# First attention of a two-layer diffusion backbone: sums of squares as two rounded matrix products

## The chip, the cores and the metric

The kernel runs on one core of one Trainium2 chip. The metric is the device time of one execution in microseconds (us), as the median over several runs. One core has TensorE (PE, matrix products into PSUM), VectorE (DVE), ScalarE (ACT), GpSimd (POOL, which works on SBUF only), and SyncE (SP), which issues the DMAs. Each engine has a queue of its own that it works through in order, and engines wait for each other by semaphores.

## What is computed

The model has two layers. The first one mixes 1024 latent tokens and 256 context tokens by multi-head attention with 12 heads beside a Fourier mixing; the second by windowed attention beside pooling. After each comes a gated convolutional FFN. The change touches the first attention alone. What it computes per head is, cut to what matters:

```python
kv = (rmsnorm(ckv, ckv_g) @ w_ukv).reshape(B, L, A_HEADS, A_NOPE + A_V)
k = jnp.concatenate([kv[..., :A_NOPE], broadcast(k_rope)], axis=-1)    # 64 + 32 = 96 entries
k = rmsnorm(k, k_g)
q = rmsnorm((rmsnorm(cq, cq_g) @ w_uq).reshape(B, L, A_HEADS, A_QK), q_g)
q, k = rope_tail(q, cos, sin), rope_tail(k, cos, sin)
p = softmax(q @ k.T * A_QK ** -0.5)      # over context and latent keys
o = p @ v
```

So each head needs, for each of its 1280 keys and 1280 queries, the sum of 96 squares (the mean in `rmsnorm`). This sum over partitions is a matrix product with a matrix of ones.

## The kernel before, in words

Function `heads0` holds the first attention. The tokens lie along the free dimension, in three chunks `CH` of 512, 512 and 256 columns. A head is worked off in 11 passes u = 0 to 10 of half-steps v = 2u and 2u + 1. In pass u TensorE computes the logits of the next 128 keys against 1024 queries (`qk`, lines 2423 to 2425: two blocks of 512 columns, each as three products of halves that are rounded to the type fp32r: high x high, high x low, low x high), ScalarE takes the exponentials (line 2629), GpSimd adds them up (`add`, lines 2400 to 2405), and TensorE multiplies them with the values (`pv`, line 2455, in plain float32). The three exponential buffers `pr[u % 3]` come free when both `pv` and `add` of their pass are done.

Between this work, in half-steps 2 to 18, the same engines prepare the *next* head, in steps that `steps_at(v)` names. There are six pieces w = 0 to 5: three chunks of keys (w < 3), three of queries. For each piece:

- `project` (TensorE, lines 2492 and 2496, plain float32): keys or queries in PSUM bank `PB[w]`.
- `project` (ScalarE): for keys a scaled copy `kx` (line 2577) and the square `sk` (2579), for queries the square `sq` (2586), for w = 5 also a plain copy (2584).
- `squares` (TensorE, line 2506, plain float32): ones x squares into bank `NB[w % 2]`.
- `inverse` (ScalarE): logarithm (2595), then exponential with factor -0.5 (2598), so the inverse root, back into the bank.
- `unit` (VectorE, 2675, 2687 and 2690, 2681): the normed result, with the rotation for queries, whose first part is `turn` (2698, 2701) and reads the projection in PSUM.
- `high` (ScalarE, 2606) rounds the result to fp32r, `low` (VectorE, 2709) takes the rest, `cast` (GpSimd, 2393) makes a bfloat16 copy.

Then come the maxima (half-steps 9 to 17): TensorE forms rough logits in bfloat16 (lines 2525, 2528 and 2534), in banks `MB`, VectorE takes 26 row maxima of them per head (2725), and a last product (2539) turns the maxima into a row (half-step 18), which ScalarE copies into a spare row of the queries (2620). The softmax of the next head can start only then.

Step n of the preparation does on TensorE `project(n)`, then `squares(n-1)`; on ScalarE `high(n-2)`, `project(n)`, `inverse(n-1)`; on VectorE `low(n-2)`, `turn(n)` for n = 3 and 4, `unit(n-1)`. Step n lies in half-step n + 2. Head 0 is prepared ahead of the loop, with the same steps and no attention beside them; heads 1 to 11 within heads 0 to 10. At the start of each head from head 1 on, `spread` (2471, 2475) and `inverse_sum` (ScalarE, 2321 and 2323) form the inverse softmax sums of the head before, and `finish` (VectorE, 2331) writes its output, all ahead of the preparation on these queues.

## Time and profile before

| | us |
|---|---|
| three runs, median (lowest to highest) | 3049.51 (3048.3 to 3057.88) |
| the profiled execution, its own time | 3050.67 |
| its span in the trace | 3048.9 |
| TensorE busy in the span | 2911.8 |
| VectorE, ScalarE, GpSimd busy in the span | 1811.4, 1349.0, 702.6 |
| mean granted TensorE clock, share of full speed | 0.982 |

The span is the time from the first to the last instruction. A matrix product is pipelined: the duration of one record is longer than the distance to the next record's start, so distances between starts tell what TensorE spends. A product in plain float32 shows as two records. A record of VectorE or ScalarE also overlaps with its successor unless it waits. The heads of the first attention lie between about 290 and 845 us of the span.

### The profile page before, as it was taken

The numbers are of one execution on the slowest core, as the hardware profiler recorded it, in microseconds if no ns is written. First come the engines' busy times: TensorE is split into PE (matmuls) and PEld (weight loads), VectorE is DVE, ScalarE is ACT, GpSimd is POOL, SyncE is SP. The second block draws the span as 40 slices with busy tenths as digits, with TensorE's granted clock in tenths as the row PEclk, the third lists the DMA queues.
The fourth block names the chain that finished last, engine by engine and source line by source line (L and its number), as shares of the span: only waits on it lengthen the run. The fifth ranks groups of instructions, "written<-read, shape, count | busy, mean of one in ns | idle before, by whom it ended". The sixth has DMA issues, their size and how long they took to land. (4 is left out here: it accounts for less than half of the span.)

```text
span 3048.9 us, 38038 instructions
## 1 busy us (share of the span) xinstructions
PE 2911.8 (96%) x13994; PEld 2106.6 (69%) x13994; DVE 1811.4 (59%) x2476; ACT 1349.0 (44%) x2138; POOL 702.6 (23%) x509
## 2 busy tenths in 40 slices
PE   5998999999999999999999999969999999999999
PEld 2563444444478888889998887834548788888887
DVE  5124655556536888888863444346653878887442
ACT  4014565655624444446652432136662544445231
POOL 0002555555610233330000000034550133331000
PEclk9998999999999999999999999979999999999999
DMA  9920000000030222225664431032211122224453
GB/s 380 375 93 2 5 3 4 4 2 2 7 117 29 83 83 83 83 83 175 189 206 126 143 102 49 35 73 65 59 46 48 64 83 83 83 83 148 137 171 100
DMA packets 101750, 282.86 MB, mean 93 GB/s; under 512 B 12129, under 2 KB 27745, under 8 KB 94562
## 3 DMA queue, kind: packets, MB, share of 16 engines
q1 hardware_dynamic: 101602, 280.88, 28.4%
q8 instruction: 94, 1.54, 0.2%
q14 instruction: 54, 0.44, 0.0%
HBM read 237.97 MB, written 27.26 MB: 87 GB/s over the span
## 5 line engine op out<-in xcount | busy, mean ns | idle before, releaser
L1370 ACT ACTIVATE z_wh<-part 128x512 fp32r<-128x512 f32 x266 | 166.3, 629 | 337.1 <-PE PS L1241 194.3
L1746 DVE TENSOR_TENSOR z_wdl<-part,z_wdh 128x512 fp32r<-128x512 f32 (+3 forms) x208 | 148.8, 721 | 256.5 <-ACT z_wdh L1423 256.3
L1241 PE MATMUL PS<-s_uh,z_wl 128*128 128x512 f32 x736 | 286.6, 389 | 0.0
L1240 PE MATMUL PS<-s_ul,z_wh 128*128 128x512 f32 x736 | 286.5, 389 | 0.0
L1239 PE MATMUL PS<-s_uh,z_wh 128*128 128x512 f32 x736 | 286.4, 389 | 0.0
L1423 ACT ACTIVATE z_wdh<-part 128x512 fp32r<-128x512 f32 (+3 forms) x208 | 135.3, 655 | 303.1 <-DMA part<-in_w_down 302.0
L2403 POOL TENSOR_TENSOR X<-X 128x1024 f32<-128x1024 f32 x96 | 229.3, 2388 | 63.1 <-ACT X L2629 62.2
L1667 DVE TENSOR_TENSOR z_wl<-part,z_wh 128x512 fp32r<-128x512 f32 x266 | 218.4, 833 | 34.4 <-ACT z_wh L1370 34.4
L1226 POOL TENSOR_TENSOR part<-part,part 128x512 f32<-128x512 f32 x38 | 56.5, 1487 | 775.1 <-DMA part<-in_w_up 775.1
L2629 ACT ACTIVATE X<-PS 128x512 f32<-128x512 f32 x252 | 145.0, 593 | 143.0 <-PE PS L2425 135.6
L2725 DVE TENSOR_REDUCE part<-PS 128x1 f32<-128x512 f32 (+1 forms) x312 | 161.8, 579 | 17.1 <-PE PS L2528 16.3
L1239 PEld LDWEIGHTS PS<-s_uh,z_wh 128*128 128x128 f32 x736 | 138.2, 188 | 29.1
L1240 PEld LDWEIGHTS PS<-s_ul,z_wh 128*128 128x128 f32 x736 | 138.1, 188 | 28.8
L1241 PEld LDWEIGHTS PS<-s_uh,z_wl 128*128 128x128 f32 x736 | 138.1, 188 | 28.8
L3173 POOL MEMSET part<- 64x1024 bf16 (+1 forms) x5 | 5.0, 1041 | 626.2 <-POOLq L137 626.2
L2455 PE MATMUL PS<-X,part 128*64 128x512 f32 x480 | 139.9, 622 | 0.0
L1239 PE MATMUL PS<-z_gh,z_wdh 128*128 128x512 f32 x352 | 137.3, 390 | 0.0
L1240 PE MATMUL PS<-z_gl,z_wdh 128*128 128x512 f32 x352 | 137.0, 389 | 0.0
L1241 PE MATMUL PS<-z_gh,z_wdl 128*128 128x512 f32 x352 | 136.9, 389 | 0.0
L3496 DVE TENSOR_REDUCE part<-PS 128x1 f32<-128x640 f32 (+1 forms) x96 | 75.6, 789 | 85.2 <-PE PS L3289 84.5
L2423 PE MATMUL PS<-h_qh,h_kh 128*128 128x512 f32 (+1 forms) x264 | 123.8, 469 | 0.9 <-ACT h_qh L2620 0.9
L1701 DVE SCALAR_TENSOR_TENSOR part<-PS,part,part 128x1023 f32<-128x1023 f32 x88 | 113.0, 1284 | 3.1
(410 smaller groups left out, 7565.9 us busy)
## 6 DMA issues: line engine op xcount, KB each, us to landing
part<-in_w_up SPq DMA_DIRECT2D x132, 512.0 KB, 3.6
part<-in_mod_w SPq DMA_DIRECT2D x48, 1024.0 KB, 7.4
part<-in_w_down SPq DMA_DIRECT2D x96, 256.0 KB, 2.7
gated<-part SPq DMA_DIRECT2D x44, 512.0 KB, 2.6
part<-gated SPq DMA_DIRECT2D x87, 256.0 KB, 5.2
part<-in_w_down SPq DMA_DIRECT2D x32, 384.0 KB, 3.1
part<-in_w_down SPq DMA_DIRECT2D x32, 320.0 KB, 3.2
part<-in_w_down SPq DMA_DIRECT2D x48, 192.0 KB, 2.4
```

The lines of the kernel that those rows point to most:

```text
L1239: pe.matmul(bank_, w_h, x_h, start=start, stop=False, skip_group_check=further)
L1240: pe.matmul(bank_, w_h, x_l, start=False, stop=False, skip_group_check=further)
L1241: return pe.matmul(bank_, w_l, x_h, start=False, stop=stop, skip_group_check=further)
L1370: act.activation(wh[i][:, :], full[b][i], ACT.Copy).then_inc(s["hi"], 1)
L1423: act.activation(wdh[j][:, :width(e)], wd[j][:, :width(e)], ACT.Copy).then_inc(s["wdh"], 1)
L1667: dve.tensor_tensor(wl[b][i][:, :], full[b][i], wh[i][:, :].bitcast(F32), ALU.subtract)\
L1746: dve.tensor_tensor(wdl[j][:, :width(e)], wd[j][:, :width(e)], wdh[j][:, :width(e)].bitcast(F32), ALU.subtract).then_inc(s["wdl"], 1)
L2403: op = pool.tensor_tensor(ac[:, 0:SEQ], ac[:, 0:SEQ], p[:, :], ALU.add)
L2423: pe.matmul(out, kh[b][:, keys], qh[b][:, lo:hi], start=True, stop=False)
L2455: mm = pe.matmul(ps(OB, BANK, slice(64 * c, 64 * c + 64)), vs[b][:, u, :], p[:, c * BANK:(c + 1) * BANK], start=(u == 0), stop=(u == 9))
L2629: act.activation(pr[u % 3][:, i % 2 * BANK:i % 2 * BANK + BANK], ps(i % 3, BANK), ACT.Exp, scale=A_SCALE).then_inc(s["P"], 1)
L2725: dve.reduce_max(mc[:, r:r + 1], ps(MB[c], hi - lo), AX_X).then_inc(s["mc"], 1)
```

## The change

The squares are split into a part that is rounded to fp32r and the rest, and their sum is formed by two fp32r products (line 2529 of the changed kernel) with a rounded matrix of ones, `unity`, in place of one product in plain float32. For this:

- ScalarE squares from PSUM back into PSUM (w = 0, 1, 2, 5) or into SBUF (w = 3, 4) and then rounds the square in one more instruction, six per head (2607, 2619). It now waits for its own instruction before, between copy and square and between square and rounding.
- The rest is subtracted by VectorE from PSUM for w = 0, 1, 2, 5 (2747), by GpSimd from SBUF for w = 3, 4 (2402).
- All steps of `project` lie one half-step sooner (step n in half-step n + 1). On TensorE `squares` keeps its half-step, and now stands ahead of `project` there, two steps behind the projection that it needs. ScalarE's order becomes `high(n-3)`, `inverse(n-2)`, `project(n)`; VectorE's `low(n-3)`, `unit(n-2)`, `turn(n)`, the new subtraction of piece n.
- The banks of projections, sums and maxima move: `project(5)` no longer takes the bank of piece 4 but that of piece 3, and waits for `turn(3)` in place of `turn(4)`. Pieces 2 and 4 wait until the rest of the squares before them is taken from their bank.
- GpSimd's casts move: piece 0 stands between the two subtractions in pass 3, pieces 1, 2, 3 in pass 4, piece 4 in pass 5.
- Ahead of the loop, the squares of the 32 rotary rows of the keys, which are the same for all heads, are split once: ScalarE rounds them (2688) and the ones (2689), VectorE subtracts (2781), ahead of five memsets on its queue.
- The first `squares` of a head waits for `finish` of the head before the running one, as `project(1)` did.

The diff, cut to its core:

```diff
-raw, sq = [[Xf[:, rest + (2 * x + n) * BANK:rest + (2 * x + n + 1) * BANK] for n in range(2)] for x in range(2)]
-t1 = [take(BANK) for _ in range(2)]
+raw, t1 = [[Xf[:, rest + (2 * x + n) * BANK:rest + (2 * x + n + 1) * BANK] for n in range(2)] for x in range(2)]
+sql = [place(f"h0_sql{n}", o + n * BANK, BANK) for n in range(2)]
+sq = [take(BANK) for _ in range(2)]
+sqh = [place(f"h0_sqh{n}", 9088 + n * BANK, BANK) for n in range(2)]
...
+skh, skl = place("h0_skh", O_MIX + 5 * T, T), place("h0_skl", -(-o // 32) * 32, T)
+unity = place("h0_unity", 10 * A_HEADS * 64, A_QK)
...
-MB = [RB, TB, RB + 1]
-NB = [5, 7]
-PB = [RB, TB, RB, TB, RB, RB]
+MB = [RB, TB, TB + 1]
+NB = [7, 5]
+PB = [RB, RB + 1, RB, TB, RB, TB]
...
-        if 2 <= v <= 8:
-            return [("prep", v - 2)]
+        if 1 <= v <= 8:
+            return [("prep", v - 1)]
         if 9 <= v <= 16:
-            return [("prep", 7)] * (v == 9) + [("max", v - 9)]
+            return [("prep", 8)] * (v == 9) + [("max", v - 9)]
...
+        def square_low(p, w):
+            pool.wait_ge(s["sqh"], 6 * p + w + 1)
+            at_least(pool, "nt", 6 * p + w - 1)
+            pool.tensor_tensor(sql[w % 2][0:96, :], sq[w % 2][0:96, :], sqh[w % 2][0:96, :].bitcast(F32),
+                               ALU.subtract).then_inc(s["sqm"], 1)
...
         values(0)
-        for w in range(6):
+        cast(0, 0)
+        square_low(0, 3)
+        square_low(0, 4)
+        for w in range(1, 6):
             cast(0, w)
...
                 if h < LAST:
-                    for w in {3: (0,), 4: (1, 2), 5: (3, 4), 6: (5,)}.get(u, ()):
+                    if u == 3:
+                        square_low(h + 1, 3)
+                        cast(h + 1, 0)
+                        square_low(h + 1, 4)
+                    for w in {4: (1, 2, 3), 5: (4,), 6: (5,)}.get(u, ()):
                         cast(h + 1, w)
...
-            elif w == 1:
+            elif w in (2, 4):
+                pe.wait_ge(s["sql"], 4 * p + w // 2 * 2 - 1)
+            elif w == 3:
                 at_least(pe, "fin", p - 1)
             elif w == 5:
-                pe.wait_ge(s["sq"], 6 * p + 5)
-                pe.wait_ge(s["ts"], 2 * p + 2)
-            else:
-                pe.wait_ge(s["sq"], 6 * p + (w - 1 if w < 5 else w))
+                pe.wait_ge(s["sq"], 6 * p + 4)
+                pe.wait_ge(s["ts"], 2 * p + 1)
...
-            pe.wait_ge(s["sq"], 6 * p + w + 1)
+            if 3 <= w < 5:
+                pe.wait_ge(s["sqm"], 2 * p + w - 2)
+            else:
+                pe.wait_ge(s["sql"], 4 * p + min(w, 3) + 1)
+            if w == 0:
+                at_least(pe, "fin", p - 1)
             at_least(pe, "lo", 6 * p + w - 1)
-            src = sk[0:A_QK, lo:hi] if w < 3 else sq[w % 2][0:A_QK, :hi - lo]
-            pe.matmul(ps(NB[w % 2], hi - lo, slice(0, A_QK)), ones[0:A_QK, 0:A_QK], src,
-                      start=True, stop=True).then_inc(s["nt"], 1)
+            for x in (skh, skl) if w < 3 else (sqh[w % 2], sql[w % 2]):
+                part = x[0:A_QK, lo:hi] if w < 3 else x[0:A_QK, :hi - lo]
+                mm = pe.matmul(ps(NB[w % 2], hi - lo, slice(0, A_QK)), unity[0:A_QK, :], part,
+                               start=x in (skh, sqh[w % 2]), stop=x in (skl, sql[w % 2]))
+            mm.then_inc(s["nt"], 1)
...
             if kind == "prep":
+                if 1 < n < 8:
+                    squares(p, n - 2)
                 if n < 6:
                     project(p, b, use, n)
-                if 0 < n < 7:
-                    squares(p, n - 1)
...
                 act.activation(kx[0:64, lo:hi], ps(PB[w], n, slice(0, 64)), ACT.Copy,
                                scale=sml[0:64, W_G0 + 1:W_G0 + 2]).then_inc(s["rawc"], 1)
-                act.activation(sk[0:64, lo:hi], ps(PB[w], n, slice(0, 64)), ACT.Square).then_inc(s["sq"], 1)
+                act.wait_ge(s["rawc"], 4 * p + w + 1)
+                square = ps(PB[w], n, slice(0, 64))
+                act.activation(square, square, ACT.Square).then_inc(s["sq"], 1)
+                act.wait_ge(s["sq"], 6 * p + w + 1)
+                act.activation(skh[0:64, lo:hi], square, ACT.Copy).then_inc(s["sqh"], 1)
             else:
                 at_least(act, "nt", 6 * p + w - 1)
                 if w == 5:
                     act.wait_ge(s["ta"], 2 * p + 1)
                     act.activation(raw[1][0:96, :n], ps(PB[w], n, slice(0, 96)), ACT.Copy)\
                         .then_inc(s["rawc"], 1)
-                act.activation(sq[w % 2][0:96, :n], ps(PB[w], n, slice(0, 96)), ACT.Square)\
-                    .then_inc(s["sq"], 1)
+                    act.wait_ge(s["rawc"], 4 * p + 4)
+                made = ps(PB[w], n, slice(0, 96))
+                square = made if w == 5 else sq[w % 2][0:96, :n]
+                act.activation(square, made, ACT.Square).then_inc(s["sq"], 1)
+                act.wait_ge(s["sq"], 6 * p + w + 1)
+                act.activation(sqh[w % 2][0:96, :n], square, ACT.Copy).then_inc(s["sqh"], 1)
...
-                if n > 1:
-                    high(p, b, n - 2)
+                if n > 2:
+                    high(p, b, n - 3)
+                if 1 < n < 8:
+                    inverse(p, n - 2)
                 if n < 6:
                     project(p, n)
-                if 0 < n < 7:
-                    inverse(p, n - 1)
...
+        act.activation(skh[64:96, :], sk[64:96, :], ACT.Copy).then_inc(s["kh0"], 1)
+        act.activation(unity[:, :], ones[:, 0:A_QK], ACT.Copy).then_inc(s["kh0"], 1)
...
+        def square_low(p, w):
+            lo, hi = CH[w % 3]
+            n = hi - lo
+            dve.wait_ge(s["sqh"], 6 * p + w + 1)
+            if w < 3:
+                out_, h_ = skl[0:64, lo:hi], skh[0:64, lo:hi]
+            else:
+                out_, h_ = [x[w % 2][0:96, :n] for x in (sql, sqh)]
+            dve.tensor_tensor(out_, ps(PB[w], n, slice(0, 64 if w < 3 else 96)), h_.bitcast(F32),
+                              ALU.subtract).then_inc(s["sql"], 1)
...
-            if kind == "prep" and n > 1:
-                low(p, b, n - 2)
+            if kind == "prep" and n > 2:
+                low(p, b, n - 3)
+            if kind == "prep" and 1 < n < 8:
+                unit(p, b, n - 2)
             if kind == "prep" and 3 <= n < 5:
                 turn(p, n)
-            if kind == "prep" and 0 < n < 7:
-                unit(p, b, n - 1)
+            if kind == "prep" and n in (0, 1, 2, 5):
+                square_low(p, n)
...
+        dve.wait_ge(s["kh0"], 1)
+        dve.tensor_tensor(skl[64:96, :], sk[64:96, :], skh[64:96, :].bitcast(F32), ALU.subtract).then_inc(s["kh0"], 1)
```

The order on ScalarE while head 1 is prepared within head 0, from one pair of exponentials (L2629 before, L2661 now) on. `part_...` are buffers in SBUF, PS is PSUM, `h_kh` the rounded keys, `h_skh` and `h_sqh` the rounded squares. Before:

```order
L2629 ACTIVATE X<-PS 128x512 x2
L2606 ACTIVATE h_kh_1468<-PS 96x512
L2577 ACTIVATE X<-PS,sml 64x256
L2579 ACTIVATE X<-PS 64x256
L2595 ACTIVATE part_1475<-PS,eps 96x512
L2598 ACTIVATE PS<-part_1475 96x512
L2606 ACTIVATE h_kh_1468<-PS 96x512
L2586 ACTIVATE X<-PS 96x512
L2595 ACTIVATE part_1475<-PS,eps 96x256
L2598 ACTIVATE PS<-part_1475 96x256
L2629 ACTIVATE X<-PS 128x512 x2
```

Now:

```order
L2661 ACTIVATE X<-PS 128x512 x2
L2638 ACTIVATE h_kh_1468<-PS 96x512
L2627 ACTIVATE part_1479<-PS,eps 96x512
L2630 ACTIVATE PS<-part_1479 96x512
L2617 ACTIVATE part_1476<-PS 96x512
L2619 ACTIVATE h_sqh_1478<-part_1476 96x512
L2638 ACTIVATE h_kh_1468<-PS 96x512
L2627 ACTIVATE part_1479<-PS,eps 96x256
L2630 ACTIVATE PS<-part_1479 96x256
L2617 ACTIVATE part_1475<-PS 96x512
L2619 ACTIVATE h_sqh_1477<-part_1475 96x512
L2661 ACTIVATE X<-PS 128x512 x2
```

Between the two pairs of exponentials stood the projections of pieces 2 and 3 (L2577 with L2579, and L2586); now the squares of pieces 3 and 4 stand there (L2617), each with its rounding (L2619), and behind the inverse roots.

The order on TensorE at the projection of piece 5 (`128x256 x2`) in the same head. Before:

```order
L2455 MATMUL PS<-X,part_1471 64x512 x2
L2496 MATMUL PS<-part_58,part_60 128x256 x2
L2506 MATMUL PS<-X,cst 96x512
L2423 MATMUL PS<-h_qh_1463,h_kh_1467 128x512
L2424 MATMUL PS<-h_ql_1465,h_kh_1467 128x512
L2425 MATMUL PS<-h_qh_1463,h_kl_1469 128x512
L2423 MATMUL PS<-h_qh_1463,h_kh_1467 128x512
L2424 MATMUL PS<-h_ql_1465,h_kh_1467 128x512
L2425 MATMUL PS<-h_qh_1463,h_kl_1469 128x512
L2506 MATMUL PS<-X,cst 96x256
L2455 MATMUL PS<-X,part_1471 64x512 x2
L2528 MATMUL PS<-part_56 128x512 x2
```

Now, with the projection one half-step sooner (`h_unity` is the rounded matrix of ones, L2529 stands for L2506):

```order
L2529 MATMUL PS<-h_sqh_1478,h_unity 96x512
L2529 MATMUL PS<-h_sql_1474,h_unity 96x512
L2513 MATMUL PS<-part_58,part_60 128x256 x2
L2472 MATMUL PS<-X,part_1471 64x512 x2
L2529 MATMUL PS<-h_sqh_1477,h_unity 96x512
L2529 MATMUL PS<-h_sql_1473,h_unity 96x512
L2440 MATMUL PS<-h_qh_1463,h_kh_1467 128x512
L2441 MATMUL PS<-h_ql_1465,h_kh_1467 128x512
L2442 MATMUL PS<-h_qh_1463,h_kl_1469 128x512
L2440 MATMUL PS<-h_qh_1463,h_kh_1467 128x512
L2441 MATMUL PS<-h_ql_1465,h_kh_1467 128x512
L2442 MATMUL PS<-h_qh_1463,h_kl_1469 128x512
```

Each sum of squares (L2506) has become a pair of L2529, and the projection of piece 5 now stands behind the sums of piece 3, and ahead of `pv` of pass 3.

The order on VectorE at the start of `heads0`. Before:

```order
L2734 MEMSET h_kh_1468 32x1280
L2734 MEMSET h_kl_1470 32x1280
L2734 MEMSET h_qh_1464 32x1280
L2734 MEMSET h_ql_1466 32x1280
L2736 MEMSET h_kh_1468 1x1280
L2675 TENSOR_TENSOR PS<-X,PS 96x512
L2709 TENSOR_TENSOR h_kl_1469<-PS,h_kh_1467 96x512
L2675 TENSOR_TENSOR PS<-X,PS 96x512
L2709 TENSOR_TENSOR h_kl_1469<-PS,h_kh_1467 96x512
```

Now:

```order
L2781 TENSOR_TENSOR h_skl<-X,h_skh 32x1280
L2783 MEMSET h_kh_1468 32x1280
L2783 MEMSET h_kl_1470 32x1280
L2783 MEMSET h_qh_1464 32x1280
L2783 MEMSET h_ql_1466 32x1280
L2785 MEMSET h_kh_1468 1x1280
L2747 TENSOR_TENSOR h_skl<-PS,h_skh 64x512 x2
L2709 TENSOR_TENSOR PS<-X,PS 96x512
L2747 TENSOR_TENSOR h_skl<-PS,h_skh 64x256
L2754 TENSOR_TENSOR h_kl_1469<-PS,h_kh_1467 96x512
L2709 TENSOR_TENSOR PS<-X,PS 96x512
L2732 SCALAR_TENSOR_TENSOR X<-PS,sml,part_58 96x512
```

One subtraction over 1280 columns stands ahead of the memsets, and two more over 512 ahead of the first normed keys.

## Rows read from the trace of the kernel before

**Rows 1.** Windows: busy us (instructions) per engine, granted TensorE clock, DMA; projections to first maximum
```profile
344.60:367.70 23.10, 22.48 (x76) 10.33 (x74) 12.90 (x21) 17.95 (x37) 11.54 (x10) 1.00 0.03 8
```

**Rows 2.** Timeline, TensorE, one head: start, us, line, tiles, count, [idle before <-releaser]
```profile
349.01 0.40 PE L2424 MATMUL PS<-h_ql,h_kh 128*128 128x512 f32 x1
349.24 0.39 PE L2425 MATMUL PS<-h_qh,h_kl 128*128 128x512 f32 x1
...
350.82 1.10 PE L2506 MATMUL PS<-X,cst 96*96 96x512 f32 x2
351.85 1.08 PE L2455 MATMUL PS<-X,part 128*64 128x512 f32 x4
...
360.72 1.13 PE L2496 MATMUL PS<-part,part 128*128 128x256 f32 x4 [0.47 <-DVE X L2701]
...
367.27 0.28 PE L2525 MATMUL PS<-part 96*128 96x256 bf16 x1
368.82 0.39 PE L2528 MATMUL PS<-part 96*128 96x512 bf16 x1 [1.27 <-DVE part L2725]
```

**Rows 3.** Timeline, ScalarE, the same head
```profile
343.52 0.71 ACT L2323 ACTIVATE PS<-part 128x640 f32<-128x640 f32 x1
...
349.01 0.68 ACT L2595 ACTIVATE part<-PS,eps 96x512 f32<-96x512 f32 x1
349.72 0.60 ACT L2598 ACTIVATE PS<-part 96x512 f32<-96x512 f32 x1
350.25 1.06 ACT L2629 ACTIVATE X<-PS 128x512 f32<-128x512 f32 x2
351.21 0.59 ACT L2606 ACTIVATE h_kh<-PS 96x512 fp32r<-96x512 f32 x1
351.69 0.46 ACT L2577 ACTIVATE X<-PS,sml 64x256 f32<-64x256 f32 x1
```

**Rows 4.** Groups by line and shape, ScalarE: count, busy us, mean ns, idle before
```profile
L2577 ACT ACTIVATE X<-PS,sml 64x512 f32<-64x512 f32 x24 | 16.4, 682 | 11.9 <-PE PS L2492 11.9
L2586 ACT ACTIVATE X<-PS 96x512 f32<-96x512 f32 x24 | 14.3, 594 | 4.4 <-PE PS L2496 4.4
L2579 ACT ACTIVATE X<-PS 64x512 f32<-64x512 f32 x24 | 13.9, 578 | 0.0
```

**Rows 5.** Timeline, VectorE: first maxima of that head
```profile
368.09 3.13 DVE L2725 TENSOR_REDUCE part<-PS 128x1 f32<-128x512 f32 x6
```

**Rows 6.** Groups by line and shape, GpSimd
```profile
L2403 POOL TENSOR_TENSOR X<-X 128x1024 f32<-128x1024 f32 x96 | 229.3, 2388 | 63.1 <-ACT X L2629 62.2
L2405 POOL TENSOR_TENSOR X<-X 128x256 f32<-128x256 f32 x12 | 8.7, 726 | 2.8 <-ACT X L2629 2.8
```

**Rows 7.** Timeline, VectorE, preparation of head 0 ahead of the loop
```profile
256.96 0.69 DVE L2675 TENSOR_TENSOR PS<-X,PS 96x512 f32<-96x512 f32 x1
...
275.21 12.96 DVE L2725 TENSOR_REDUCE part<-PS 128x1 f32<-128x512 f32 x26
```

**Rows 8.** Timeline, TensorE: the bf16 rows of three heads, the third with half clock inside
```profile
383.44 0.72 PE L2539 MATMUL PS<-identb,part 128*1 128x128 bf16 x10 [0.55 <-DVE part L2731]
430.81 0.72 PE L2539 MATMUL PS<-identb,part 128*1 128x128 bf16 x10 [0.54 <-DVE part L2731]
479.88 0.72 PE L2539 MATMUL PS<-identb,part 128*1 128x128 bf16 x10 [0.56 <-DVE part L2731]
```

**Rows 9.** Timeline, TensorE, where the third of these heads begins its maxima
```profile
463.57 0.39 PE L2528 MATMUL PS<-part 96*128 96x512 bf16 x1 [1.22 <-DVE part L2725]
...
464.71 1.98 PE L2455 MATMUL PS<-X,part 128*64 128x512 f32 x4
```

**Rows 10.** Windows, just behind the wait of rows 9
```profile
464.80:468.10 3.30, 3.30 (x9) 1.04 (x10) 2.00 (x5) 0.00 (x0) 1.59 (x1) 0.50 0.00 0
```

**Rows 11.** Timeline, TensorE, preparation of head 0
```profile
259.15 0.64 PE L2506 MATMUL PS<-X,cst 96*96 96x256 f32 x2 [2.38 <-DVE h_kl L2709]
259.63 3.30 PE L2496 MATMUL PS<-part,part 128*128 128x512 f32 x4
```

More of the change, by code:

```diff
@@ L2305, in heads0 @@
                      ("one", "one1", "pad", "pad1", "S", "P", "PV", "raw", "rawc",
-                      "sq", "nt", "ln", "rinv", "t1", "ts", "ta", "out", "hi", "lo", "cast", "vs", "mx", "mc", "mn", "mrow",
+                      "sq", "sqh", "sql", "sqm", "kh0", "nt", "ln", "rinv", "t1", "ts", "ta", "out", "hi", "lo", "cast", "vs", "mx", "mc", "mn", "mrow",
                       "mr", "o", "bc", "lnr", "rs", "fin", "ad")}
```

## Prediction

> **What bounds the kernel now.** I read the windows first: in the 23.1 us of one head in which the next is prepared, from the first projection to the first row maximum, TensorE is busy 22.48, ScalarE 17.95, VectorE 12.90, GpSimd 11.54 us [rows 1]. TensorE sets the pace, but ScalarE has only 5.15 us of slack, and each piece passes through it three times. The timeline of TensorE then shows where it waits in that stretch: 0.47 us ahead of the projection of piece 5, for `turn(4)`, and 1.27 us at the first maxima [rows 2]. That second wait is the end of a chain on ScalarE and VectorE: VectorE's first maximum starts only at 368.09, behind the last `low` [rows 5], and TensorE goes on at 368.82. From there on the head is fixed by TensorE with VectorE just behind it. So the change is worth what it moves that start of the maxima, and not what it takes off TensorE.
>
> A second thing stands in the rows of three heads: the bf16 row comes 47.37 us after the one before, then 49.07 us [rows 8]. In the longer head the same kind of wait (1.22 us) is followed by matrix products of twice the duration (`pv` 1.98 against 1.08 us) [rows 2, 9], with a granted clock of 0.50, so 1.2 GHz instead of 2.4 [rows 10]. I found this in 2 of the 10 heads whose rows can be compared. It costs 1.6 to 1.7 us each.
>
> **The change, part by part.**
>
> *TensorE, sums.* One float32 sum over 512 columns takes 1.03 us to the next start, an fp32r product 0.23 [rows 2], so two take 0.46. Saved: 0.57 for each of four pieces, half of it (an estimate by columns) for two, 2.85 us per head. Changes between number types take back a part that these rows don't separate; I take 2.4, with 2.0 and 2.85 as ends. The 0.47 us of wait at piece 5 goes as well, since `turn(3)` is done long before. What is late next is ScalarE.
>
> *ScalarE.* It gets six roundings per head and waits for itself in ten places. The prices: a copy or square in a row without a wait starts its successor about 0.1 us before its end, one with a wait 0.03 behind it (351.21 to 351.69 for a 0.59 us copy; 349.01 to 349.72 for a 0.68 us logarithm) [rows 3]. The work from its first `project` to the last `high`, in start-to-start distances: keys 512, copy 0.71, square 0.61, rounding 0.49, twice, 3.6; keys 256, 1.2; queries 512, 0.62 + 0.49, twice, 2.2; queries 256 with its raw copy, 1.1; four inverse roots at 1.24 (349.01 to 350.25) and two at 0.8, 6.6; six `high`, 2.5; four pairs of exponentials at 0.96, 3.8 [rows 3, 4]. Figures for 256 columns are these less 0.2 for the columns, as the 0.46 us copy shows against 0.68. Sum 21.0 us. It begins when `inverse_sum` has ended at 343.52 + 0.71 = 344.23 [rows 3] and the first projection, now right behind the first `pv`, has landed, by my count at 344.65. Two waits stay inside: about 0.3 us for VectorE ahead of the raw copy of piece 5, and 0.6 for the last `unit`; some 0.2 lie between items. Last `high` ends at 366.9, the last `low` and the first maximum follow 0.4 later: 367.3 against 368.09. **Gain 0.8 us per head, 11 heads, 8.7 us.** Ends: 0.1 (the same count from the busy time: 17.95 + 2.5 for roundings + 1.3 for the lost overlap = 21.75) and 1.4 (no wait left inside).
>
> *TensorE's wait.* It arrives earlier than the maxima: the second block of logits in pass 6 needs the exponential of pass 5, which ScalarE now makes at about 364.1, and ends near 365.7; TensorE goes on at 368.82 - 0.8 = 368.0. The wait of 1.27 us becomes 2.1.
>
> *VectorE* gets four subtractions, 0.69 us for 512 columns [rows 7], 2.2 us per head. It has 10 us free in the stretch [rows 1]; those ahead of `unit` fall into time in which it waits for ScalarE. If that cover were gone they would add up to 2.2. The wait of the first `squares` for `finish` costs nothing: `finish` used to be awaited in the same half-step, by a projection.
>
> *GpSimd* gets two subtractions. It has 2.39 us for 1024 columns and 0.73 for 256 [rows 6], so 1.3 us each. In pass 3 it now waits for the rounding of piece 4 (about 358.0) with `add(3)` queued behind, which then ends near 361.7. The exponentials of pass 6 need it, and start near 367: 5 us of margin. If it were late, each us late would be one us of head. The casts of keys are done by 363.3, just ahead of the first maxima. The Trainium skill, "GPSIMD Engine Reference", section "Key points", says that GpSimd shares its SBUF interfaces with VectorE and contends with VectorE instructions that have two SBUF inputs; by that the two subtractions could be slower where `unit` adds from SBUF, which the margin would take up, so the sum stays. No row here shows a slowdown.
>
> *DMA and SP.* The weight loads of a head are issued one half-step sooner; nothing waits for them in these rows, nothing is added.
>
> *Head 0*, ahead of the loop. VectorE does `unit` of piece 0 at 256.96, right behind its memsets, and the first maximum at 275.21 [rows 7]. The new subtraction over 1280 columns (an estimate by columns: 1.5 us) waits for a rounding by ScalarE (about 1 us) and stands ahead of the memsets: 2.5 us. Two subtractions of 0.69 then come ahead of the first `unit`, partly covered. I take **3.4 us**, with 1.5 and 6 as ends.
>
> *The clock.* A wait of 1.2 to 1.3 us was followed by half clock in 2 of 10 heads. In the preparation of head 0 a wait of 2.38 us was followed by half clock at once (four records of the projection in 3.30 us, rows 11). Mine, 2.1, lies two thirds of the way between; I put 8 of 11 heads, 6 more than now, at 1.65 us [rows 8]: **9.9 us lost**. Ends: none more (0) and all 11 (14.9). Against this stands the Trainium skill, "TensorE: Matmul & The Clock Gate", section "HAM oscillation — how this bites in real kernels", which has only long idle gaps bring the clock down, longer than any here; by it nothing is lost and the sum is 3044. The half clock behind 1.22 us [rows 9, 10] speaks against taking it as it stands.
>
> **Sum.** -8.7 + 3.4 + 9.9 = +4.6 us. The profiled execution took 3050.67 us, 1.2 above the median of the three runs; against the median the forecast is 3049.5 + 4.6 = **3054 us**, which is within 0.3% (9.1 us, so 3040.4 to 3058.7), about what a measurement of this kernel can tell from no change.
>
> **Rivals.**
>
> 1. *The clock stays at 2.4 GHz about as often as now.* Then -8.7 + 3.4: 3044 us. For it: 8 of 10 waits of 1.2 us had no effect. Against: rows 11. Chance 0.20.
> 2. *Slower: half clock in every head.* Place: behind the wait at the first maxima. Price 1.65 us in each of 9 more heads, 14.9 us. It decides from a wait of some 2.4 us on [rows 11], so if the wait grows 0.3 more than I count. With the gain of 8.7 that is 3049.5 - 8.7 + 3.4 + 14.9 = 3059 us, and 3067 if ScalarE's chain is no shorter than now. Chance 0.24.
> 3. *ScalarE does not bind*, because its items pack more tightly beside TensorE, and the whole saving on TensorE goes through: 11 x (2.4 + 0.47) = 31.6 less 3.4: 3021 us. Against: 21 us of work behind 344.65 cannot end before 365.7. Half of it would be 3035. Chance 0.07.
> 4. *The change doesn't do what it says on TensorE*: the fp32r pair, with its own weights of ones, takes as long as the float32 sum. Then TensorE arrives as now, the wait shrinks to 0.5, and the clock no longer falls: -8.7 + 3.4 - 3.3 = 3041 us. Against: the fp32r rows beside it at 0.23 [rows 2]. Chance 0.03.
>
> The forecast itself has 0.46 (3048 to 3058).
>
> **Numbers.** Faster by over 0.3%: rival 3 and parts of 1 and 4, 0.14. Slower by over 0.3%: most of rival 2, 0.22. Within: 0.64. The range takes in the forecast, rival 1 with the upper end of ScalarE's gain, and rival 2 up to its middle: 3038 to 3064 us.
>
> **What would show it.** In the changed profile: two L2529 records of 512 columns 0.23 us apart; no wait ahead of the projection of piece 5; ScalarE nearly without idle time from the first projection to the last `high`; the wait of TensorE for VectorE's first maximum at 2.1 us (wrong if under 1.5 or over 2.6); 46.6 us from row to row in heads at full clock, 48.2 in the others, and 8 of these; head 0's first maximum 3.4 us later behind the start of `heads0`. The prediction is wrong if idle time on ScalarE exceeds 2 us in that stretch, or if the heads with half clock are as few as now.

## The result, and the profile after

| | before | changed |
|---|---|---|
| median of the runs, us | 3052.4 (4 runs, 3048.3 to 3057.88) | 3098.56 (4 runs, 3089.62 to 3100.92) |
| ratio, 95% interval | | **1.0142 [1.0121, 1.0163]** |
| profiled execution: own time, span, us | 3050.67, 3048.9 | 3089.62, 3087.8 |
| mean granted TensorE clock | 0.982 | 0.973 |
| busy TensorE, VectorE, ScalarE, GpSimd, us | 2911.8, 1811.4, 1349.0, 702.6 | 2913.7, 1880.8, 1384.0, 737.3 |

The change makes the kernel slower: by 46 us between the medians, by 37 to 50 us by the interval. The forecast was 3054 us, with a range up to 3064. VectorE is busy 69 us more. Its new subtractions, 2.2 us in each of twelve preparations and 1.5 once, are 28 of them. The trace of the changed kernel is of its fastest run, 9 us below its median, so the two traces differ by less than the medians.

The bf16 rows of TensorE give the heads. Two of them in the changed kernel, as in [rows 8]:

```profile
345.52 0.72 PE L2563 MATMUL PS<-identb,part 128*1 128x128 bf16 x10 [0.56 <-DVE part L2778]
...
397.24 0.72 PE L2563 MATMUL PS<-identb,part 128*1 128x128 bf16 x10 [0.56 <-DVE part L2778]
```

The distance is 51.72 us. Over all eleven heads the mean is 51.42, against 47.69 before; 50.1 at full clock against 47.4. Head 0's row comes at 292.77 instead of 288.51. 11 x 3.73 + 4.3 = 45.3 us. Behind the last row 6.3 us come back (2229.5 us from there to the end against 2235.7), in a stretch that the change doesn't touch and that lay between 2229 and 2240 in all traces of this study. That makes the 38.9 us between the two spans.

Where in a head does it go? The groups of waits from 290 to 880 us (total, times, longest):

```profile
PE PS L2529 <- DVE h_ql L2754: 31.6, 11, 2.9
...
PE PS L2552 <- DVE part L2772: 21.4, 22, 1.8
...
ACT h_qh L2638 <- DVE PS L2724: 23.0, 11, 2.1
...
ACT X L2612 <- DVE X L2721: 20.3, 11, 1.9
```

The same list of the kernel before has only these on that path:

```profile
PE PS L2528 <- DVE part L2725: 15.9, 22, 1.3
...
ACT h_qh L2606 <- DVE PS L2690: 16.8, 11, 1.6
```

So ScalarE, which was to run nearly without a pause, waits for VectorE twice per head, 1.9 and 2.1 us, and TensorE waits 2.9 us ahead of the sum of piece 5. VectorE, which was to have 10 us to spare, is what both wait for. Its timeline in the head of rows 1 to 5, now from the projection of piece 5 on:

```profile
369.02 2.53 DVE L2721 TENSOR_TENSOR X<-X 32x512 f32<-32x512 f32 x1
371.59 0.69 DVE L2724 TENSOR_TENSOR PS<-X,PS 96x512 f32<-96x512 f32 x1
...
373.29 0.69 DVE L2754 TENSOR_TENSOR h_ql<-PS,h_qh 96x512 fp32r<-96x512 f32 x1
374.01 2.78 DVE L2721 TENSOR_TENSOR X<-X 32x512 f32<-32x512 f32 x1
376.82 0.69 DVE L2724 TENSOR_TENSOR PS<-X,PS 96x512 f32<-96x512 f32 x1
...
380.22 2.20 DVE L2772 TENSOR_REDUCE part<-PS 128x1 f32<-128x512 f32 x4
```

L2721 is the second half of the rotation, an addition over 32 partitions and 512 columns with both inputs in SBUF (L2687 before). It takes 2.53 and 2.78 us. The operation by itself, over all heads (min/median/max ns), after and before:

```profile
L2721 DVE TENSOR_TENSOR X<-X x24: 682/2542/2787, 271.8 to 835.3; 32x512 f32<-32x512 f32 x24
```

```profile
L2687 DVE TENSOR_TENSOR part<-part,X x24: 682/683/721, 266.6 to 793.2; 32x512 f32<-32x512 f32 x24
```

And GpSimd at the same time:

```profile
367.38 1.27 POOL L2402 TENSOR_TENSOR h_sql<-part,h_sqh 96x512 fp32r<-96x512 f32 x1 [0.61 <-ACT h_sqh L2619]
368.61 2.40 POOL L2413 TENSOR_TENSOR X<-X 128x1024 f32<-128x1024 f32 x1
370.94 1.43 POOL L2397 CAST part<-h_kh 96x512 bf16<-96x512 f32 x2
...
373.89 2.35 POOL L2413 TENSOR_TENSOR X<-X 128x1024 f32<-128x1024 f32 x1
```

Its two float32 additions (L2413) start at 368.61 and 373.89, 0.41 and 0.12 us ahead of VectorE's. VectorE ends 0.54 and 0.55 us behind the end of GpSimd's (371.55 against 371.01, 376.79 against 376.24), as if it had only begun there. The 1.85 and 2.10 us above 0.68, in eleven heads, are 43 us; with the 28 above that is 71, near the 69 measured. In the kernel before, the same head has its GpSimd addition sooner (VectorE, then GpSimd):

```profile
360.70 0.72 DVE L2687 TENSOR_TENSOR part<-part,X 32x512 f32<-32x512 f32 x1
```

```profile
358.52 2.35 POOL L2403 TENSOR_TENSOR X<-X 128x1024 f32<-128x1024 f32 x1
```

VectorE starts 0.17 us ahead of GpSimd's end, and ends 0.55 behind it, so there it loses only 0.04 us. TensorE of the changed kernel, in the same head as above:

```profile
360.03 0.40 PE L2529 MATMUL PS<-h_skh,h_unity 96*96 96x512 f32 x1
360.26 0.40 PE L2529 MATMUL PS<-h_skl,h_unity 96*96 96x512 f32 x1
...
367.21 1.03 PE L2513 MATMUL PS<-part,part 128*128 128x256 f32 x4
...
374.12 0.33 PE L2529 MATMUL PS<-h_sqh,h_unity 96*96 96x256 f32 x1 [2.88 <-DVE h_ql L2754]
...
380.96 0.39 PE L2552 MATMUL PS<-part 96*128 96x512 bf16 x1 [1.76 <-DVE part L2772]
...
382.10 1.89 PE L2472 MATMUL PS<-X,part 128*64 128x512 f32 x4
```

The pair of L2529 is 0.23 us apart and the projection of piece 5 (367.21) waits for nothing, as forecast. Then come 2.88 us of wait, and the first maximum (380.22) lies 34.70 us behind the head's row, where it was 32.07 (368.09 - 336.02): 2.63 us later instead of 0.8 sooner. The head at full clock is 2.7 us longer, the same amount. Finally the clock, in windows over the two stretches of matrix products with longer durations:

```profile
376.80:378.50 1.70, 1.70 (x5) 1.32 (x4) 1.02 (x2) 0.95 (x2) 0.30 (x1) 0.50 0.00 0
382.10:385.00 2.90, 2.90 (x9) 0.74 (x9) 1.69 (x4) 0.00 (x0) 1.66 (x1) 0.52 0.00 0
```

Half clock, 1.2 GHz, comes twice in nearly every head: once behind the 2.88 us, in all 11, where TensorE must wait again anyway, and once behind the wait at the first maxima, in 9 of the 11, where it costs about 1.5 us (the two heads without it last 50.1 us, the others 51.4 to 51.7, the first 52.75).

### The profile page after: what moved, and what is told of

Its sections match the earlier page's. It is cut to its first block and busy times, and to the rows that moved or that the text cites. A ratio compares the mean times of both kernels' runs of the same rounds, so it can differ in the third digit from the quotient of the medians.

```text
span 3087.8 us, 38279 instructions
## 1 busy us (share of the span) xinstructions
PE 2913.7 (94%) x13994; PEld 2110.9 (68%) x13994; DVE 1880.8 (61%) x2525; ACT 1384.0 (45%) x2212; POOL 737.3 (24%) x533
## 5 line engine op out<-in xcount | busy, mean ns | idle before, releaser
L2413 POOL TENSOR_TENSOR X<-X 128x1024 f32<-128x1024 f32 x96 | 229.7, 2392 | 90.4 <-ACT X L2661 89.5
L1667 DVE TENSOR_TENSOR z_wl<-part,z_wh 128x512 fp32r<-128x512 f32 x266 | 219.7, 837 | 34.7 <-ACT z_wh L1370 34.7
L2661 ACT ACTIVATE X<-PS 128x512 f32<-128x512 f32 x252 | 143.1, 591 | 148.9 <-PE PS L2442 142.5
L2472 PE MATMUL PS<-X,part 128*64 128x512 f32 x480 | 150.6, 669 | 0.0
```

The costliest lines, as they stand in the source:

```text
L1667: dve.tensor_tensor(wl[b][i][:, :], full[b][i], wh[i][:, :].bitcast(F32), ALU.subtract)\
L2413: op = pool.tensor_tensor(ac[:, 0:SEQ], ac[:, 0:SEQ], p[:, :], ALU.add)
L2472: mm = pe.matmul(ps(OB, BANK, slice(64 * c, 64 * c + 64)), vs[b][:, u, :], p[:, c * BANK:(c + 1) * BANK], start=(u == 0), stop=(u == 9))
L2661: act.activation(pr[u % 3][:, i % 2 * BANK:i % 2 * BANK + BANK], ps(i % 3, BANK), ACT.Exp, scale=A_SCALE).then_inc(s["P"], 1)
```

## The experiments

The theory after these rows: **VectorE's addition with two SBUF inputs can't run while GpSimd's float32 addition runs, and stands still until that ends.** The rivals: the new place of the buffers in SBUF slows the operation; the number of GpSimd's instructions does; or the clock is the cause and the wait its consequence. All ratios are against the kernel before, run on the same chip in the same session: median 3053.7 us (25 runs) for experiments 1, 2, 3 and 5, 3054.4 (25 runs) for 6 to 9, 3053.4 (11 runs) for 4, 10 and 11. "Behind the row" is the distance from the bf16 row that begins a head.

### 1. The new places of the buffers, alone

The kernel before, with `t1` and the squares exchanged as in the change:

```diff
-raw, sq = [[Xf[:, rest + ...] ...] ...]
-t1 = [take(BANK) for _ in range(2)]
+raw, t1 = [[Xf[:, rest + ...] ...] ...]
+sq = [take(BANK) for _ in range(2)]
```

> The kernel before, with t1 moved into X beside raw and sq moved out of it, as the change does, and nothing else. Theory 'port' (VectorE's add with both inputs in SBUF cannot run beside GpSimd's float32 add, and the change moved GpSimd's queue under it): the add of the rotated part (L2687) stays at 0.68 to 0.72 us, total 3050 us, no change. Theory 'place' (it is slow since both inputs now lie in X, where GpSimd and ScalarE work too): about 2.5 us in heads 1 to 11, 3.9 us more per head, some 3090 us.

Measured: 3056.2 us, ratio 1.0 [0.9988, 1.0012]. The addition stays at 0.68 to 0.72 us, the heads at 47.4 (49.0 in the three with half clock). It isn't the place.

### 2. GpSimd's order

The changed kernel, with the two subtractions and the cast of piece 0 behind `add(3)` instead of ahead of it:

```diff
-if u == 3:
+if u == 4:
     square_low(h + 1, 3)
     cast(h + 1, 0)
     square_low(h + 1, 4)
-for w in {4: (1, 2, 3), 5: (4,), 6: (5,)}.get(u, ()):
+for w in {4: (1, 2), 5: (3, 4), 6: (5,)}.get(u, ()):
```

> The changed kernel, with GpSimd's two subtractions and the cast of piece 0 behind add(3) instead of ahead of it, and the cast of piece 3 behind add(4). Port: the VectorE add L2721 of piece 3 falls from 2.53 to 0.7 us, that of piece 4 from 2.78 to between 0.7 and 2.0, since add(4) now starts about 370.0 instead of 373.9; 3055 to 3075 us. Place: both stay at 2.5 and 2.8, 3098 us.

Measured: 3072.2 us, ratio 1.0059 [1.0043, 1.0076]. Piece 4 is free again, but piece 3 is worse than in the change. VectorE, then GpSimd:

```profile
368.32 3.42 DVE L2721 TENSOR_TENSOR X<-X 32x512 f32<-32x512 f32 x1
...
374.19 0.68 DVE L2721 TENSOR_TENSOR X<-X 32x512 f32<-32x512 f32 x1
```

```profile
367.91 0.95 POOL L2397 CAST part<-h_kh 96x512 bf16<-96x512 f32 x2
368.82 2.38 POOL L2413 TENSOR_TENSOR X<-X 128x1024 f32<-128x1024 f32 x1
```

I had expected piece 3 to be free (0.7 us) and piece 4 at 0.7 to 2.0. That the time lies in the expected range is therefore chance. `add(3)` now runs early, but the addition of piece 3 falls upon two casts and, right behind them, `add(4)`. VectorE starts 0.41 us behind the first cast and ends 0.54 behind the end of `add(4)` (371.20): it is held through three instructions of GpSimd in a row, 3.42 us. The time follows: first maximum at 33.48 us behind the row, heads of 48.9 and some 50.0.

### 3. One GpSimd addition moved onto VectorE's, in the kernel before

If one float32 addition is enough, the stall can be made without any part of the change. `add(4)` is held back until `turn(4)` is done:

```diff
+if u == 4:
+    pool.wait_ge(s["ts"], 2 * (h + 1) + 2)
 add(h, u)
```

> The kernel before, with one wait more: GpSimd's add(4) is held until VectorE has done turn of piece 4, so that it runs beside the VectorE add L2687 of piece 3. Port: that add grows from 0.70 to between 2.2 and 2.7 us, in heads 1 to 11, piece 4 stays at 0.68; the first maximum comes 1.6 to 2 us later per head: 3070 us, more if the clock falls oftener. Place: 0.7 us as before, 3050 us; the hold alone costs nothing, as the exponentials that need add(4) come 7 us later.

Measured: 3056.0 us, ratio 1.0007 [0.9992, 1.0021]: a miss. VectorE's addition stays at 0.68 us. VectorE, then GpSimd:

```profile
363.20 0.68 DVE L2689 TENSOR_TENSOR part<-part,X 32x512 f32<-32x512 f32 x1
```

```profile
363.25 2.86 POOL L2403 TENSOR_TENSOR X<-X 128x1024 f32<-128x1024 f32 x1 [2.27 <-DVE X L2703]
```

But now VectorE starts 0.05 us ahead, and it is GpSimd's addition that takes 2.86 us instead of the 2.37 it has elsewhere. The one that starts first keeps the other out; here GpSimd has time to lose. So the theory needs the order of the two starts, and the next run of it reverses that order.

### 4. The same, 0.8 us sooner

`add(4)` held only until the first rotated part (`t1`) is there, so that it starts ahead of VectorE's addition:

```diff
+if u == 4:
+    pool.wait_ge(s["t1"], 2 * (h + 1) + 2)
 add(h, u)
```

> The kernel before, with GpSimd's add of piece 4 held only until VectorE has the t1 of its turn(4) done, so that it starts some 0.8 us ahead of VectorE's 32x512 add of piece 3 (two SBUF inputs) instead of 0.05 us behind it. Theory (whoever starts first keeps the other out): that VectorE add takes 2.2 to 2.5 us instead of 0.69 in each of the 11 heads, GpSimd's add stays at 2.37, the first maximum comes some 1.6 us later behind the bf16 row, and the time is 3065 to 3080. Rival (it is the change's subtractions and roundings on GpSimd, or their number, that slow VectorE, not a single float32 add): the add stays at 0.7 us and the time at 3050 to 3056.

Measured: 3074.1 us, ratio 1.0069 [1.0047, 1.0091]. VectorE, then GpSimd:

```profile
364.98 2.15 DVE L2689 TENSOR_TENSOR part<-part,X 32x512 f32<-32x512 f32 x1
```

```profile
364.24 2.34 POOL L2403 TENSOR_TENSOR X<-X 128x1024 f32<-128x1024 f32 x1 [1.48 <-DVE part L2700]
```

One wait that moves one GpSimd instruction by 0.8 us against experiment 3 makes the addition 2.15 us long, ending 0.55 us behind GpSimd's (366.58), in all 11 heads. The first maximum moves from 32.0 to 33.45 us behind the row, the full-clock head from 47.4 to 48.85, and 6 heads have half clock instead of 2. Nothing of the change is in this kernel: the stall is shown by itself, at 1.45 us of head for 1.47 us of stall. The granted clock is 1.00 while VectorE stands still here (364.98 to 367.13 us), so the clock isn't what makes it wait.

### 5. The same addition with one input in PSUM

In the changed kernel the instruction gets an input from PSUM in place of the one in SBUF. It multiplies by the inverse root, which lies in PSUM, so the second rotated part is left out and the rotation is incomplete. Its size and successors stay, but it now waits for the inverse root.

```diff
-dve.tensor_tensor(t_[64:96], t_[64:96], raw[w % 2][64:96, :n], ALU.add).then_inc(s["ta"], 1)
-dve.wait_ge(s["ta"], v + 1)
 dve.wait_ge(s["rinv"], 6 * p + w + 1)
+dve.tensor_tensor(t_[64:96], t_[64:96], norm_[64:96], ALU.mult).then_inc(s["ta"], 1)
+dve.wait_ge(s["ta"], v + 1)
```

> The changed kernel, where the VectorE add L2721 reads one input from SBUF and one from PSUM (it multiplies by the inverse root instead of adding the second rotated part, so the rotation of queries is left incomplete) and comes behind the wait for the inverse root. Port: 0.69 us beside GpSimd's running add, the wait of TensorE ahead of the sum of piece 5 falls from 2.88 us to under 0.7, and the head to 46.6 us at full clock as forecast: 3050 to 3060 us. Place: still 2.5 us, 3098 us.

Measured: 3065.8 us, ratio 1.0048 [1.0033, 1.0062]. The operation, in all 24 places:

```profile
L2722 DVE TENSOR_TENSOR X<-X,PS x24: 684/685/686, 277.7 to 805.3; 32x512 f32<-32x512 f32 x24
```

One of them starts at 371.26 in the middle of a GpSimd addition (370.03 to 372.43) and takes 0.69. So do all 22 of the loop: each starts while a GpSimd addition still has over 1.1 us to run. So an input in PSUM frees it. The time missed the expected 3050 to 3060, and the head the expected 46.6: heads last 47.5 at full clock. VectorE now waits for the inverse root ahead of this instruction, 0.85 and 0.58 us in the head above; that this is what keeps the gain of the change away was not tried by itself, but experiment 6, without that wait, has the gain.

### 6. The change without the stall

The second rotated part goes back into its own PSUM bank, and is added at once in `turn`, so that the addition has one input in PSUM. The projection of piece 5 waits for this addition, since it takes the bank.

```diff
-pe.wait_ge(s["ts"], 2 * p + 1)
+pe.wait_ge(s["ta"], 2 * p + 1)
...
-dve.wait_ge(s["ts"], v + 1)
-dve.tensor_tensor(t_[64:96], t_[64:96], raw[w % 2][64:96, :n], ALU.add).then_inc(s["ta"], 1)
...
-dve.scalar_tensor_tensor(out=raw[w % 2][64:96, :n], in0=ps(PB[w], n, slice(96, P)),
+dve.wait_ge(s["t1"], 2 * p + w - 2)
+dve.scalar_tensor_tensor(out=ps(PB[w], n, slice(64, 96)), in0=ps(PB[w], n, slice(96, P)),
                          ...
+dve.wait_ge(s["ts"], 2 * p + w - 2)
+t_ = t1[w % 2][64:96, :n]
+dve.tensor_tensor(t_, t_, ps(PB[w], n, slice(64, 96)), ALU.add).then_inc(s["ta"], 1)
```

> The changed kernel, where the second rotated part of a query (turn, L2735) stays in PSUM, in its own bank, and is added right there, so that no VectorE instruction of the preparation reads twice from SBUF; project(5) waits for that add. The sum stays the reference's. Port: every such add takes 0.69 us, the two waits that grew (sum of piece 5: 2.88 us, raw copy of piece 5: 1.84 us) fall to under 1.2 and 0.3, the head at full clock goes from about 50.0 to 46.6 to 47.3 us. With half clock behind the first maxima in 4 to 9 heads at 1.65 us, and 4.3 us for head 0: 3050 to 3062 us. Rival (the chain through ScalarE is itself longer than I counted, by its waits for its own instructions): heads stay at 48.5 us or more, 3070 us.

Measured: 3054.6 us, ratio 0.9995 [0.9982, 1.0007]. That is 44 us below the change. It is also the number that was forecast for the change, but only by luck: the forecast stood 4.6 us above the kernel before, and this version stands level with it, at most 2 us above by the interval. The addition (L2739) is 0.69 us long in all 24 places, and in 11 of them GpSimd's float32 addition has 1.7 us still to run. The first maximum lies 31.0 us behind the row, 1.05 sooner than before. ScalarE, from its first copy to its last rounding of the preparation, is busy 20.8 of 22.2 us and idle for 1.4 (in the head of the rows below); in the kernel before it was busy 16.8 of 21.5 and idle for 4.7. So ScalarE has little left to give in this stretch. Heads last 46.4 us at full clock; 7 of 11 have half clock (six of 48.0, the first of 48.7). From the waits of TensorE between 290 and 880 us (total, times, longest), the two that make up its loss in a head:

```profile
PE PS L2552 <- DVE part L2774: 15.1, 23, 1.2
...
PE PS L2529 <- DVE h_kl L2756: 11.2, 22, 0.6
```

TensorE at the first maxima of a head with half clock:

```profile
380.02 0.28 PE L2549 MATMUL PS<-part 96*128 96x256 bf16 x1
381.45 0.39 PE L2552 MATMUL PS<-part 96*128 96x512 bf16 x1 [1.15 <-DVE part L2774]
...
382.59 1.76 PE L2472 MATMUL PS<-X,part 128*64 128x512 f32 x4
```

A wait of 1.15 us is followed by `pv` at 1.76 us instead of 1.08 us.

### 7. Head 0

The five memsets ahead of head 0 go from VectorE's queue, where the change puts a subtraction ahead of them, to GpSimd's, on top of 6:

```diff
+for n, x in enumerate((kh[1], kl[1], qh[1], ql[1])):
+    pool.memset(x[96:P, :].bitcast(F32), 0.0).then_inc(s["pad1"], 1)
+    pool.wait_ge(s["pad1"], n + 1)
+pool.memset(kh[1][96:97, :].bitcast(F32), 1.0).then_inc(s["one1"], 1)
...
-for n, x in enumerate((kh[1], kl[1], qh[1], ql[1])):
-    dve.memset(x[96:P, :].bitcast(F32), 0.0).then_inc(s["pad1"], 1)
-dve.wait_ge(s["pad1"], 4)
-dve.memset(kh[1][96:97, :].bitcast(F32), 1.0).then_inc(s["one1"], 1)
```

> e5 with the five memsets that stood ahead of VectorE's work for head 0 moved to GpSimd. If these and the subtraction ahead of them are what delays head 0, its bf16 row comes 6 us sooner than in e5 (292.8 in the changed kernel, so about 286.5) and the total falls by 5 to 6 us. Rival (the chain of head 0 is bound by ScalarE and the half clock): less than 2 us.

Measured: 3047.8 us, ratio 0.9975 [0.9963, 0.9987], 6.8 us below experiment 6. From the start of `heads0`, the first memset on GpSimd, to head 0's row it is 36.5 us against 42.3 in experiment 6, so the 5.9 us lie where they were expected. The heads of the loop are as there (46.4; 48.0 in 6 of 11).

### 8. Half clock taken away

On top of 7, the bf16 product that stands just ahead of the wait for the first maxima is made 12 times into the same place instead of once. It keeps TensorE at work in the wait and changes no result.

```diff
-pe.matmul(ps(MB[2], T - CH[2][0]), qb[0:A_QK, 0:P], kb[0:A_QK, CH[2][0]:T],
-          start=True, stop=True).then_inc(s["mx"], 1)
+for _ in range(12):
+    mm = pe.matmul(ps(MB[2], T - CH[2][0]), qb[0:A_QK, 0:P],
+                   kb[0:A_QK, CH[2][0]:T], start=True, stop=True)
+mm.then_inc(s["mx"], 1)
```

> e6 with the 256-column bf16 product ahead of TensorE's wait for the first maximum (L2549) made twelve times over, into the same place, with the same result: 1.3 us of work inside a wait of about 2 us. If the clock falls because TensorE waits there, no head has half clock behind the first maxima any more, every head takes 46.6 to 47.3 us, and the total falls by 1.65 us for each head that had it, 7 to 15 us below e6. Rival (the clock falls by itself now and then): as many heads with half clock as in e6, same time.

Measured: 3034.9 us, ratio 0.994 [0.992, 0.9959].

```profile
366.99 1.49 PE L2555 MATMUL PS<-part 96*128 96x256 bf16 x12
368.41 0.39 PE L2559 MATMUL PS<-part 96*128 96x512 bf16 x1
...
369.56 1.08 PE L2477 MATMUL PS<-X,part 128*64 128x512 f32 x4
```

The wait is gone, `pv` takes 1.08 us, and no head of the loop has a stretch at half clock: ten last 46.3 to 46.4 us. The first maximum is at 31.0 us behind the row as in 6 and 7, so the chain is untouched. The 11 heads together take 511.0 us against 520.9 in experiment 7: 10 of the 13 us between the medians are the clock's in these heads. The other 3 are within the intervals of the two.

### 9. The same two edits on the kernel before

Memsets on GpSimd and the 12 products, the edits of 7 and 8, put into the kernel before.

> The kernel before with the memsets on GpSimd and the same twelvefold product. Its wait is 1.27 us, so the filler fits or adds 0.1 us per head; the two heads with half clock (1.65 us each) should be gone, and head 0 ready 1 to 2 us sooner: 3045 to 3049 us. It says how much of what e7 gains belongs to the change and how much could be had without it.

Measured: 3049.9 us, ratio 0.9982 [0.9969, 0.9995], 1 us above what was expected. No half clock in the loop, ten heads of 47.3 to 47.4 us. Head 0's row comes 36.9 us behind the start of `heads0`, 1.7 sooner than in the kernel before and as in experiment 8 (36.8). Against experiment 8 the heads are 1.0 us longer: with stall and half clock out of both kernels, that is what the change is worth per head, 11 us of the 15 between the two medians. For the other 4, a trace of each doesn't settle where they lie.

### 10. Without the filler products in head 0

```diff
-for _ in range(12):
+for _ in range(1 if isinstance(p, int) and p == 0 else 12):
```

> The corrected version with the memsets on GpSimd and the filler products in heads 1 to 11 only, not in head 0, where they cost some 1.9 us: theory (fillers keep the clock, and head 0 has no need of them) 3031 to 3035, heads of 46.3 to 46.4 us without half clock. Rival (head 0's or head 1's clock falls without them and gives it back): 3035 to 3037.

Measured: 3033.6 us, ratio 0.9938 [0.9919, 0.9958]. This has the lowest median of the study, some 20 us below the kernel before. The step from 8 lies inside both intervals, so what it brings is not shown.

### 11. The filler products in the changed kernel, with its stalls

The edit of 10 alone, in the changed kernel.

> The changed kernel with the filler products alone, in heads 1 to 11, and with its two waits for GpSimd left as they are. Theory (port first, clock a follower): the VectorE adds stay at 2.5 and 2.8 us, the heads come down from 51.7 to 50.0 us in the 9 heads whose second half clock goes, so 12 to 15 us below the change, 3084 to 3087. Rival (the wait of 2.9 us ahead of the sum of piece 5 brings the half clock all the same, behind the fillers): 3095 to 3100.

Measured: 3082.6 us, ratio 1.0098 [1.0075, 1.0122], 16 us below the change (12 to 15 were expected). The first maximum stays at 34.7 us behind the row and the full-clock head at 50.1 us; of the spread above it little is left (10 heads last 50.0 to 50.5). TensorE:

```profile
376.39 0.50 PE L2529 MATMUL PS<-h_sqh,h_unity 96*96 96x256 f32 x1 [2.85 <-DVE h_ql L2756]
...
377.04 1.98 PE L2472 MATMUL PS<-X,part 128*64 128x512 f32 x4
...
382.34 1.78 PE L2550 MATMUL PS<-part 96*128 96x256 bf16 x12
...
384.86 1.08 PE L2472 MATMUL PS<-X,part 128*64 128x512 f32 x4
```

The 2.85 us of wait are there, and half clock behind them too (`pv` 1.98 at 377.04), in 8 places of the loop; but TensorE waits again behind this stretch, and when the maxima start (`pv` 1.08 at 384.86) the clock is full. So the stall costs by itself, and the clock is a second, smaller loss that follows it.

## Why the prediction was wrong

**The step that failed is the paragraph on GpSimd**, and with it the price of VectorE's addition. The prediction asked only whether GpSimd would be late (5 us of margin), let a slower GpSimd be taken up by that margin, and closed with "so the sum stays. No row here shows a slowdown". That VectorE could be the one to wait was not priced: its addition, which the change leaves as it is, kept the 0.68 us it had. It took 2.53 and 2.78 us. What moved it into the collision is the order that the prediction described itself: the two subtractions and a cast stand ahead of `add(3)`, which therefore starts at 368.61, just before VectorE reaches piece 3; and `add(4)`, queued behind, does the same to piece 4. Experiment 2 changes this order alone and frees piece 4, while piece 3 meets `add(4)`. Before the change VectorE's 24 additions all missed GpSimd's, or began within its last 0.2 us (0.68 to 0.72 us long then).

The sentence was true of the rows that I had read and false of the trace. Two other places of the kernel before have the stall. VectorE's subtraction over 1280 columns at the end of the block, 1.48 us undisturbed (VectorE, then GpSimd):

```profile
L606 DVE TENSOR_TENSOR out_l<-part,out_h x16: 1210/1480/3608, 824.1 to 2287.5; 128x1280 fp32r<-128x1280 f32 x8, 128x1024 fp32r<-128x1024 f32 x8
```

```profile
824.12 6.22 DVE L606 TENSOR_TENSOR out_l<-part,out_h 128x1280 fp32r<-128x1280 f32 x2 [0.77 <-ACT out_h L602]
```

```profile
823.00 2.40 POOL L2403 TENSOR_TENSOR X<-X 128x1024 f32<-128x1024 f32 x1 [1.30 <-ACT X L2629]
825.61 20.38 POOL L2403 TENSOR_TENSOR X<-X 128x1024 f32<-128x1024 f32 x7 [0.22 <-ACT X L2629]
```

The first of the two starts 1.1 us behind the start of a GpSimd addition, and they take 6.22 us where some 3.0 would do. And in the FFN a 0.69 us subtraction takes 1.77, ending 0.55 behind GpSimd's:

```profile
1062.50 1.77 DVE L1667 TENSOR_TENSOR z_wl<-part,z_wh 128x512 fp32r<-128x512 f32 x1
```

```profile
1061.45 2.27 POOL L1231 TENSOR_TENSOR part<-part 128x512 f32<-128x512 f32 x1
```

The longest durations of VectorE's operations with two SBUF inputs (3608 ns against a median of 1480) would have pointed to the price: the rest of GpSimd's addition, up to 2.4 us for each of the two pieces. Half of that on average (an estimate), twice in each of 11 heads, is 26 us, and if all of it is on the critical path a forecast of 3080 instead of 3054.

The rule was in the Trainium skill. The page I cited, "GPSIMD Engine Reference", names a contention; "SBUF — State Buffer", section "Who interferes with whom", which I didn't cite, says that the shared ports are an exclusive lock, that a VectorE instruction with two SBUF inputs contends with a GpSimd instruction that reads SBUF, and that the order of issue decides who blocks. The runs agree: 2.15 us where GpSimd leads by 0.74 (experiment 4), 2.86 us for GpSimd where VectorE leads by 0.05 (experiment 3), 0.69 with an input in PSUM (experiment 5).

Step by step:

- *TensorE, sums*: right. Pairs 0.23 us apart, no wait ahead of piece 5.
- *ScalarE's chain*: right in mechanism. The items of the forecast (21.0 us of work, 0.9 of waits, 0.2 between items) make 22.1 us from the first copy to the last rounding, and experiment 6, with the stall out, has 22.2. The gain was forecast at 0.8 us and is 1.05 there. (The items end at 366.75 and not at the 366.9 of the text, so the sum itself gives 0.95.) In the change itself the gain doesn't show: ScalarE waits 3.9 us for VectorE at the two places above alone, above the 2 us that the prediction named as what would make it wrong.
- *TensorE's wait at the first maxima*, 2.1 us forecast: 1.76 in the change, but with 2.88 us ahead of it that were not forecast, so its agreement is an accident. In experiment 6 it is 1.15 us, and two waits of 0.5 us ahead of the sums, which the prediction had at nothing, hold the rest.
- *VectorE*: four new subtractions are there and the 2.2 us of them don't lengthen the head of experiment 6, but the cover of 10 us was a sum over the stretch; the two stalled additions stand at its end, where ScalarE and TensorE wait for them.
- *Head 0*: 3.4 us forecast, 4.3 measured between the rows. The start of `heads0` itself lies anywhere from 249.8 to 258.7 us in the traces; measured from it, the row comes 43.0 us behind it instead of 38.5, 4.5 later. VectorE's memsets start at 252.90 instead of 250.33, 2.6 us later (2.5 forecast). Experiment 7 takes 5.9 us off by moving them.
- *The clock*: 8 heads at 1.65 us forecast. In the change 9 of 11, in experiment 6 7 of 11. Both are near the 8, but by luck: the 8 were read off a wait of 2.1 us, on a line from the waits before (1.27) to head 0's (2.38), on which 2.1 lies at three quarters and not at two thirds. The wait in experiment 6 is 1.15 us, shorter than the 1.27 that brought 2 of 11. So the length of this wait alone doesn't tell how many heads get half clock. Against the rule that only long idle gaps bring the clock down, stated in the Trainium skill ("TensorE: Matmul & The Clock Gate", section "HAM oscillation — how this bites in real kernels"), the rows of experiment 6 show it behind a wait of 1.15 us.
- *The rivals*: none named the stall. Rival 2 (half clock in every head) had the right sign; its size, at most 15 us for the clock, is near the 16 that experiment 11 takes off.

In us for the change: the head at full clock would last 46.4 without the stall (experiment 6) and lasts 50.1 with it, 11 x 3.7 = 41 for the stall; what the change gains takes back 11 x 1.0 = 11 of them, against the 47.4 before. With about 11 for seven more heads with half clock and 4.3 for head 0 this makes 45. Between the medians there are 46, but since the traces of the same code differ by several us outside these heads, the agreement to 1 us is not to be leaned on.

## What to carry to other kernels

Ask of every VectorE instruction with two SBUF inputs what GpSimd does when it starts: beside a running GpSimd instruction (float32 additions and casts here) it costs the rest of that one too. So keep one input in PSUM, or let VectorE start first where GpSimd has the time to wait. Before moving work to GpSimd, compare the longest with the median duration of such operations in the whole trace, not only in the stretch that is changed. And where a wait of some 1 us on TensorE is followed by half clock, try filler products in it, on the kernel before as well, so that the change isn't credited with what they bring.

## What the runs showed of the hardware

- The hold between GpSimd and VectorE is decided by who starts first, and by as little as 0.05 us (experiments 3 and 4). It is held over GpSimd's casts too, and it doesn't always end with one instruction: in experiment 2 VectorE stood still through two casts and an addition in a row (3.42 us), while in the changed kernel it went ahead of the casts that were queued behind the addition, which took 1.43 us for two instead of 0.95. In head 0 of the changed kernel it went ahead of the second of two casts as well (0.98 us). What decides that wasn't tried.
- With one input in PSUM the same operation took 0.68 to 0.69 us in all 24 places of experiments 5 and 6 each, beside running GpSimd additions.
- The half clock came behind waits of 1.15 to 1.27 us in some heads and not in others of the same kernel, and the shorter waits brought it more often (7 of 11 heads at 1.15 us, 2 of 11 at 1.2 to 1.27). The filler products in the wait took it away in every head of the loop (experiments 8 to 10). Which head gets it stays open.
